# Spreading attention's inverse sums through memory instead of products on PE

## The reference, cut to what matters

```python
p = jnp.exp(sc - m[..., None])
s = jnp.sum(p, axis=-1)
o = jnp.einsum('bdhnqk,bdhnke->bdhnqe', p, vs) / s[..., None]      # kind A; softmax(sc) @ v in kind B
o_c = (a[:, :, 0] - lam * a[:, :, 1]) @ v                          # kind C, a = softmax
mixed = concatenate([out_a, out_b, out_c]); return mixed @ w_out
```

## Time and profile before

| what | us |
|---|---|
| three runs, lowest, median, highest | 3278.37, 3282.98, 3284.76 |
| span of the profiled execution | 3277.8 |
| PE busy | 3212.9 (98%) |
| DVE busy | 1887.5 (58%) |
| ACT busy | 518.6 (16%) |
| POOL busy | 227.2 (7%) |

### The profile page before, as it was taken

How to read it: one execution, slowest core, us unless ns; L and a number is a source line. 1 busy time by engine, 2 the same in 40 slices (tenths; PEclk the granted TensorE clock), 3 DMA queues, 4 the chain that set the end, 5 groups by cost and what they waited for, 6 DMA issues and landing times.

```text
span 3277.8 us, 35937 instructions
## 1 busy us (share of the span) xinstructions
PE 3212.9 (98%) x14204; PEld 2555.1 (78%) x14204; DVE 1887.5 (58%) x3222; ACT 518.6 (16%) x1069; POOL 227.2 (7%) x197
## 2 busy tenths in 40 slices
PE   8999999999999999999899999999999999999998
PEld 3788845788888888884478888888888744788887
DVE  5356935665338764472767664476644637676643
ACT  3111121100001000104631000010001046310001
POOL 1244400000000000002000000000000030000000
PEclk9999999999999999999999999999999999999999
DMA  5244311222222222223012222222222230122221
GB/s 233 78 156 165 140 53 39 77 90 80 88 93 78 90 90 81 87 83 118 7 39 90 90 81 86 91 90 83 84 90 91 73 122 1 52 79 89 90 81 61
DMA packets 43063, 286.16 MB, mean 87 GB/s; under 512 B 5232, under 2 KB 5232, under 8 KB 12048
## 3 DMA queue, kind: packets, MB, share of 16 engines
q1 hardware_dynamic: 38880, 271.14, 23.5%
q0 software_dynamic: 4016, 12.73, 1.2%
HBM read 279.66 MB, written 2.10 MB: 86 GB/s over the span
## 4 chain that ended last, share of the span: by engine, by line
PE 88%; DVE 7%; DVEq 2%; ACT 1%; issue 1%; DMA 1%; SPq 0%; ACTq 0%; POOL 0%
PE ps L835 73%; PE ps L553 5%; PE ps L534 3%; PE ps L1212 2%; PE ps L1180 1%; PE ps L937 1%; DVE arena L1771 1%; DVE arena L2178 1%; ACT arena L1477 1%; DMA ring<-in_w_ada 1%; PE ps L1194 1%; DVE ring L1547 1%; DVEq L2191 0%; PE ps L1151 0%; PE ps L1144 0%
## 5 line engine op out<-in xcount | busy, mean ns | idle before, releaser
L835 PE MATMUL ps<-arena 128*128 128x256 f32 x5456 | 1245.1, 379 | 0.8 <-DVE arena L1862 0.6
L835 PEld LDWEIGHTS ps<-arena 128*128 128x128 f32 x5456 | 1036.3, 190 | 142.8 <-DVE arena L1862 1.6
L835 PE MATMUL ps<-arena,ring 128*128 128x256 f32 x2768 | 646.3, 379 | 0.5 <-ACT arena L1252 0.5
L835 PEld LDWEIGHTS ps<-arena,ring 128*128 128x128 f32 x2768 | 525.6, 190 | 72.5 <-ACT arena L1252 0.9
L835 PE MATMUL ps<-xn,ring 128*128 128x256 f32 x2272 | 521.0, 380 | 8.4 <-DVE arena L2111 3.2
L835 PEld LDWEIGHTS ps<-xn,ring 128*128 128x128 f32 x2272 | 431.8, 190 | 76.5 <-issue 8.5
L1586 DVE TENSOR_TENSOR arena<-arena,ps 128x512 f32<-128x512 f32 x169 | 116.1, 687 | 529.1 <-PE ps L835 496.9
L1562 DVE TENSOR_TENSOR arena<-ring 128x512 f32<-128x512 f32 (+1 forms) x190 | 128.4, 676 | 348.0 <-PE ps L835 347.7
L835 PE MATMUL ps<-xn,arena 128*128 128x256 f32 x1264 | 302.2, 379 | 0.0
L835 PEld LDWEIGHTS ps<-xn,arena 128*128 128x128 f32 x1264 | 240.2, 190 | 32.6
L1391 ACT ACTIVATE arena<-arena 128x512 f32<-128x512 f32 x88 | 55.5, 630 | 920.3 <-DVE arena L2056 920.3
(11 more groups left out here) (315 smaller groups left out, 2363.2 us busy)
## 6 DMA issues: line engine op xcount, KB each, us to landing
ring<-in_w_up_a SPq DMA_DIRECT2D x44, 1024.0 KB, 4.8
ring<-in_w_up_b SPq DMA_DIRECT2D x44, 1024.0 KB, 4.8
ring<-in_w_ff SPq DMA_DIRECT2D x32, 1024.0 KB, 4.9
ring<-in_w_ada SPq DMA_DIRECT2D x24, 1024.0 KB, 4.9
ring<-in_w_down_a SPq DMA_DIRECT2D x16, 1024.0 KB, 4.9
ring<-in_w_down_b SPq DMA_DIRECT2D x16, 1024.0 KB, 4.8
ring<-in_w_in SPq DMA_DIRECT2D x14, 1024.0 KB, 4.9
ring<-in_w_out SPq DMA_DIRECT2D x12, 1024.0 KB, 4.9
```

Of the source, the lines that this page charges most:

```text
L835: mm = nc.tensor.matmul(out_ap, w, operand(product, quads[i]), start=at not in opened, stop=last_chunk and i == len(quads) - 1, skip_group ...
```

## The change

The products with the identity, the copy out of the bank, and the pair's use of a turn bank go. In their place SP writes the 128x8 inverses to a small tensor in memory, `inv_rows`, of two buffers by two heads by 512 queries, number by number so that a head's queries lie in a row; when that has landed it reads each row back, broadcast to 64 partitions, into `spread_inv`. DVE's multiplication waits for the two reads.

```diff
--- before.py
+++ after.py
@@ turn_uses
-            if pair_ending(n - 4) is not None:
-                use((layer, "norm", pair_ending(n - 4)), "act")
@@ build
+        inv_rows = nc.dram_tensor("inv_rows", (2, 2, S), F32, kind="Internal").ap()
@@ SP
+            def spread_inverses(layer, j):
+
+                at = 8 * layer + j
+                sp.wait_ge(sem("inverted"), at + 1)
+                wait(sp, "mixed", at - 1)
+                by_query = inv_rows[j % 2, :, :].rearrange("u (i p) -> p u i", p=P)
+                with nc.allow_non_contiguous_dma(reason="columns of inverse sums become rows"):
+                    nc.sync.dma_start(by_query, inv_p[:, j % 2, :, :]).then_inc(sem("inverses_out"), 16)
+                sp.wait_ge(sem("inverses_out"), 16 * at + 16)
+                for u in range(2):
+                    row = inv_rows[j % 2, u:u + 1, :].to_broadcast([64, S])
+                    nc.sync.dma_start(spread_inv[64 * u:64 * u + 64, j % 2, :], row).then_inc(sem("inverses_in"), 16)
...
                 load_one("out2", A["w_out2"], 16, 4, layer)
+                for j in range(len(PAIRS)):
+                    spread_inverses(layer, j)
                 load_one("up_b", A["w_up_b"], 16, 22, layer)
@@ PE, weigh
-                    pe.wait_ge(sem("inverted"), 8 * layer + j + 1)
-                    wait_turn_bank(pe, (layer, "norm", j))
-                    for i in range(ST):
-                        for u in range(2):
-                            mm = nc.tensor.matmul(turn_bank((layer, "norm", j))[64 * u:64 * u + 64, i * P:(i + 1) * P],
-                                                  inv_p[:, j % 2, u, i:i + 1].to_broadcast([P, 64]), ident,
-                                                  start=True, stop=True)
-                    mm.then_inc(sem("turned"), 1)
@@ ACT
-                def spread(j):
-                    wait_turned(act, (layer, "norm", j))
-                    wait(act, "mixed", 8 * layer + j - 1)
-                    nc.scalar.activation(spread_inv[:, j % 2, :], turn_bank((layer, "norm", j)), ACT.Copy)\
-                        .then_inc(sem("turns_act"), 1)
...
-                    if pair_ending(n - 4) is not None:
-                        spread(pair_ending(n - 4))
@@ DVE, mix
-                    wait_turn_read(dve, (layer, "norm", j))
+                    dve.wait_ge(sem("inverses_in"), 32 * (8 * layer + j + 1))
```

## The result

The change makes the kernel slower: 3299.49 us as the median of four runs (3296.99 to 3305.48) against 3280.77 of the kernel before on the same chip, a ratio of 1.0054 with a 95% interval of 1.004 to 1.0068 (this ratio and those below are as given with the runs, and not quite the quotients of the medians). The prediction was 3270.0. The profiled execution spans 3295.3 us, 17.5 more than before.

A forecast was written before the change was run, and what follows sets the result against it. PE was taken to bound attention, with the inverses' products in its chain of waits. Profiled span 3277.8 - 13.0 removed + 5.2 (median above span) = 3270.0 us, the trip hidden; range 3263 to 3283.

The forecast's parts named there:

- What goes: In attention, PE's products that spread the inverses leave the chain of waits: 12.2 us plus 0.8, sum 13.0 us.
- ACT's copy at nothing: ACT loses 16 copies of 128x512 in attention, costed at no gain because ACT idles before the one shown.
- The round trip: Store to memory and two broadcast reads between reciprocal and multiplication: 9.5 us, 6.2 of it the store, fitting every room.
- upper bound: Longest trip allowed by the rows: 13.6 us, with a store of 10.3 us at 0.13 us a packet.
- overruns: Trip time beyond a pair's room before DVE's multiplication; at 13.6 us some 4.6 us over both layers, leaving 8.4 gained.
- The cover of the last pair: At each layer's end, PE's output projection lets the last multiplication start 13.8 us after the reciprocal's end before PE waits.
- The third rival: Slower: the store outlasts its bounds and DVE stands at every pair's multiplication; 3303.6 us with a 17 us trip; chance 0.14.

The follow-up runs named there:

- e4: The kernel before without the identity products, ACT's copy and bank uses, nothing in their place; 3271.06 us, ratio 0.9967, stage change -12.5 us.
- e1: The kernel before, products and copy kept, plus the stores of single numbers, without reads; 3308.99 us, ratio 1.0082, stage change +25.6 us.
- e8: The changed kernel with six products of constants put on PE ahead of the scores of step 13; 3299.41 us, ratio 1.0055.
- e10: The changed kernel with five products of constants put on PE ahead of the scores of step 12; 3314.93 us, ratio 1.0099.
- e5: The kernel before plus stores of the inverses as 128 rows of 32 bytes, products and copy kept; 3281.06 us, ratio 0.9999.
- e6: The kernel before plus the stores of single numbers, except the second pair's in each layer; 3284.93 us, ratio 1.0004.

## Why the prediction was wrong

- **What goes: right.** 13.0 us forecast, 12.5 by e4's stage (10.1 by its median). ACT's copy at nothing fits that sum too.
- **The round trip: mis-sized.** The store was taken at 6.2 us and took 10.2, by the upper bound's own arithmetic (a price per packet from the earlier trace rows). From the end of the reciprocal (1605.64) to the multiplication (1620.04) the fourth pair took 14.4 us, 13.8 of it in the store and the reads; over both layers the eight trips that DVE waited for took 13.5 to 15.1, where the prediction's upper bound was 13.6 and its choice 9.5. At 13.6 it put the overruns at 0.2, 1.5 and 0.6 us for the second, fourth and sixth pair; 0, 2.19 and 0.48 were measured. This is of the size of the 4 us that e1 and e4 leave over, and not the cause of the loss.
- **The cover of the last pair: right, with nothing to spare.** Its wait of 4.74 us passes beside the projection's products; that of 5.78 in the second layer just exceeds the cover.
- **The step that failed:** "None of this uses PE. So the question is whether the round trip is shorter than the room between the reciprocal and the multiplication." I asked only who waits for the new transfers, and never which other transfer is under way beside them. The sum had no term for that, and it was the largest: 25.6 us by e1. The sign lay in the trace before: the reciprocal that releases the second store stands at 1556.02, and POOL issues the layer's last window at 1556.40 and already waits 0.77 us for it. So a delay of it goes on to POOL and DVE, and what exceeds PE's work in hand to PE: 10.32, 10.37 and 6.66 us.
- **The third rival had the sign and not the mechanism.** It wanted trips of over 14.7 us and DVE standing at every multiplication. But DVE waited at eight of the sixteen multiplications only, two of their trips were as long (15.1 and 14.75, both in the second layer, the latter the last pair's), and DVE's long stand is at the minima that need the window, not at a multiplication. That its 3303.6 lies near the 3299.49 measured is luck. The Trainium skill's rule that a strided last dimension makes one descriptor per element ("DMA: Bandwidth & Descriptors", Rules for kernel authors) agrees with the trace: 17,152 more packets under 512 bytes, 16 x 1024 of them these numbers. I weighed it only as the price of the store itself.
- **The clock was no term either.** Behind the stand it is at 0.50, and that is some 4 of the 11.2 us that this pair of the first layer loses against e4 (from the scores behind the second weighing to those behind the third: 1590.41 - 1565.69 = 24.72 us against 1576.72 - 1563.19 = 13.53).

## What to carry to other kernels

Price a new transfer twice: by what waits for it, and by what else is in flight in the microseconds in which it is issued, above all where one engine's neighbouring instructions release both. Count its packets before its bytes: 4 KB in 1024 pieces cost this kernel 25.6 us by the neighbour they held up, and in 128 pieces nothing that could be measured. If the layout forces single numbers, turn the data on chip first; a 128x8 transpose or a 32x32 turn a pair was far cheaper than the wait.

## What the runs showed of the hardware

- A store of 1024 single numbers of 4 bytes lands in 10.2 us (8.3 to 12.0), the same 4 KB as 128 rows of 32 bytes in 1.4 (at most 3.4).
- A window issued behind such a store fares worst. In the four kernels where a 512 KB window on POOL's queue is issued 0.15 or 0.16 us behind the store on SP's (the changed one, e1, e8, e10), it lands in 13.0 to 14.1 us in both layers, against 3.6 to 3.8 in the kernel before, e5 and e6. Windows issued up to 0.6 us ahead of such a store land in 3.4 to 11.7 us.
- After PE had waited 6.66 us the granted clock was 0.50 for some 12 us, though PE was busy throughout. In e10 it fell as far behind 2.44 us of idling, with 4.56 us of products ahead of it in the same stand; in the changed kernel it stayed at 1.00 behind 2.50 us of idling ahead of 1623.52. So the length of the idling alone does not tell.
